# Two transformer blocks on one core: the taps of a 31-wide convolution become tiles of the weight stream

## The reference

```
u = rms_norm_2(h, norm_mix[i])
q, k, v, c, g = jnp.split(u @ w_in[i], splits, axis=-1)
... y_attn = window_attention(q, k, v, ...) @ w_attn_out[i]
c_val, c_gate = jnp.split(c, 2, axis=-1)
c = c_val * jax.nn.sigmoid(c_gate)                     # 256 tokens x 512 channels
c = depthwise_conv(c, conv_w[i], conv_b[i])            # 31 taps, each channel by itself
c = jax.nn.silu(layer_norm_2(c, conv_ln_g[i], conv_ln_b[i]))
y_conv = c @ w_conv_out[i]
g_attn, g_conv = jnp.split(jax.nn.sigmoid(g), 2, axis=-1)
h = h + (g_attn * y_attn + g_conv * y_conv) @ w_o[i]
```

## Time and profile before

| | us |
|---|---|
| median of three runs | 2175.07 (2174.5 to 2175.16) |
| profiled execution | 2176.42 |
| its span | 2174.4 |
| DVE busy | 1677.5 (77%) |
| ACT busy | 1263.8 (58%) |
| hi copies, 656, ACT | 689.0, 1.056 each |
| lo splits, 656, DVE | 792.9, 1.221 each |

### The profile page before, as it was taken

The page is one execution under the profiler, slowest core; times in us unless marked ns, Lnnn a source line. Parts: engine busy times, 40 slices in busy tenths (PEclk is TensorE's granted clock), DMA queues, the critical chain, the costliest instruction groups (busy, mean ns, idle before and its releaser), DMA issues.

```text
span 2174.4 us, 38816 instructions
## 1 busy us (share of the span) xinstructions
PE 2153.4 (99%) x16094; PEld 1967.3 (90%) x16094; DVE 1677.5 (77%) x2610; ACT 1263.8 (58%) x2098; POOL 13.1 (1%) x20
## 2 busy tenths in 40 slices
PE   8999999999999999999999999999999999999999
PEld 6898989999998998998888999988898889998888
DVE  7877599888876678877787677888678766978875
ACT  4754656555745556555555557665565545676554
POOL 0000000000000000000000000000000000000000
PEclk9999999999999999999999999999999999999999
DMA  9544566777644467655555533555555553355553
GB/s 363 200 163 170 171 232 244 246 242 274 225 146 165 138 232 223 211 176 188 181 188 192 179 123 117 203 187 192 186 181 188 191 185 135 119 165 206 189 189 131
DMA packets 116370, 415.12 MB, mean 191 GB/s; under 512 B 13105, under 2 KB 16561, under 8 KB 115682
## 3 DMA queue, kind: packets, MB, share of 16 engines
q1 hardware_dynamic: 116194, 412.63, 56.2%
HBM read 409.42 MB, written 3.16 MB: 190 GB/s over the span
## 4 chain that ended last, share of the span: by engine, by line
PE 93%; DVE 3%; ACT 2%; DMA 2%; issue 0%; SPq 0%; ACTq 0%
PE bank L198 92%; DMA raw<-W 2%; DVE lo L205 1%; ACT arena L250 1%; PE bank L202 1%; DVE arena L205 1%; ACT hi L250 0%; DVE arena L213 0%; DVE ada L222 0%; ACT L242 0%; DMA xT<-x 0%; ACT L250 0%; DVE h L205 0%; DVE ysl L205 0%; DVE sml L231 0%
## 5 line engine op out<-in xcount | busy, mean ns | idle before, releaser
L198 PE MATMUL bank<-h,hi 128*128 128x256 f32 (+1 forms) x5344 | 1223.1, 314 | 0.0
L250 ACT ACTIVATE hi<-raw 128x1024 fp32r<-128x1024 f32 x656 | 689.0, 1056 | 568.7 <-PE bank L198 500.6
L198 PE MATMUL bank<-h,lo 128*128 128x256 f32 x3440 | 986.2, 287 | 3.7 <-DVE h L205 3.6
L198 PEld LDWEIGHTS bank<-h,hi 128*128 128x128 f32 x5344 | 880.1, 190 | 67.1 <-issue 2.6
L205 DVE TENSOR_TENSOR lo<-raw,hi 128x1024 fp32r<-128x1024 f32 x656 | 792.9, 1221 | 92.6 <-ACT hi L250 91.8
L198 PEld LDWEIGHTS bank<-h,lo 128*128 128x128 f32 x3440 | 654.6, 190 | 15.8 <-issue 7.3
L198 PE MATMUL bank<-act,hi 128*128 128x512 f32 x1056 | 370.0, 393 | 0.0
L198 PE MATMUL bank<-act,lo 128*128 128x256 f32 x1056 | 294.7, 279 | 0.0
L198 PEld LDWEIGHTS bank<-act,hi 128*128 128x128 f32 x1056 | 197.9, 187 | 47.1
L198 PEld LDWEIGHTS bank<-act,lo 128*128 128x128 f32 x1056 | 197.9, 187 | 0.0
L198 PE MATMUL bank<-arena 64*64 64x64 f32 (+7 forms) x2674 | 196.9, 271 | 1.0 <-ACT arena L250 0.6
(11 more groups left out here) (150 smaller groups left out, 1915.9 us busy)
## 6 DMA issues: line engine op xcount, KB each, us to landing
raw<-W SPq DMA_DIRECT2D x664, 512.0 KB, 3.3
ada<-WA SPq DMA_DIRECT2D x80, 512.0 KB, 3.7
arena<-WA SPq DMA_DIRECT2D x16, 512.0 KB, 14.4
p_projected<-arena SPq DMA_DIRECT2D x2, 1024.0 KB, 7.8
arena<-scr SPq DMA_DIRECT2D x16, 128.0 KB, 4.9
arena<-p_projected SPq DMA_DIRECT2D x2, 1024.0 KB, 5.4
xT<-x SPq DMA_DIRECT2D x2, 512.0 KB, 5.1
arena<-lora SPq DMA_DIRECT2D x2, 512.0 KB, 9.8
```

The lines of the kernel that those rows point to most:

```text
L198: return self.done(lambda e: e.matmul(out, l, r, start=start, stop=stop, skip_group_check=True))
L250: return self.done(lambda e: e.activation(out, in_, f, scale=scale, **kw))
```

## The change

The 88 PE taps of the two layers become 88 tiles of the weight stream, two runs of 22 a layer. The host lays the 128 weights of a tap on the diagonal of a 128x128 tile; the tile comes by DMA and is split like any other. The values are split as well: ACT copies 266 columns of `Cb` to `Ch`, DVE writes the rest to `Cl`. ACT's diagonals and PE's float32 taps go. The order of the DVE taps stays; the sum for the first pair of groups comes at step 8, the one for the second pair after step 20. The runs stand in the main list, the first behind the factor column and the second between the last qkv group and v. A layer has 44 tiles, five and a half blocks, so between the first layer's runs and the second layer's the block borders lie four tiles off. On ACT the attention's chain is no longer put to the front.

```diff
+TW = S + CW - CV - 1
-NT2 = 2 * (44 * 8 + 22 * 8) + 30 * 8 + 32 + 32 + 64 + 64 + 16
+NT2 = 2 * (44 * 8 + 22 * 8) + 30 * 8 + 32 + 32 + 64 + 64 + 16 + 4 * 11
 def conv2_steps(l):
     for pair in (0, 2):
-        todo = [(m, j) for m in (pair, pair + 1) for j in range(CV, CW)]
-        built = []
         for j in range(0, CV, 2):
-            s += [("taps", pair, j)]
-            if j >= 4:
-                s += [("pe tap", pair, *t) for t in built.pop(0)]
-            built.append(todo[:3])
-            del todo[:3]
-            s += [("diag", pair, *t) for t in built[-1]] + ["next"]
-        s += [("conv sum", pair)]
+            s += [("taps", pair, j)] + [("conv sum", 0)] * ((pair, j) == (0, 14)) + ["next"]
+    s += [("conv sum", 2)]
...
-        s += [("mixer2", l), ("c", l, 0), ("c", l, 1), ("c", l, 2), ("conv2", l), ("c", l, 3), ("c last", l), ("rcol", l)]
-        s += [("qkv", l, p) for p in range(3)] + [("v2", l), ("qk norm", l), ("attention2", l)]
+        s += [("mixer2", l), ("c", l, 0), ("c", l, 1), ("c", l, 2), ("conv2", l), ("tap halves", l, (0, 1)), ("c", l, 3),
+              ("c last", l), ("rcol", l), ("taps", l, 0)]
+        s += [("qkv", l, p) for p in range(2)] + [("tap halves", l, (2, 3)), ("qkv", l, 2), ("taps", l, 2), ("v2", l), ("qk norm", l), ("attention2", l)]
...
+                elif what == "taps":                     # TensorE
+                    l, pr = q
+                    o = take(CONV, ("conv", l, pr))
+                    for m in (pr, pr + 1):
+                        pe.wait_ge(v_cv, ("tap halves", l, m))
+                        for j in range(CV, CW):
+                            wh, wl, ends = tile([("conv_w_2", l, j, ("diag", m))])
+                            om = t256(o, m - pr)
+                            ch, cl = (x[m % 3][:, j - CV:j - CV + 256] for x in (Ch, Cl))
+                            pe.mm(om, wl, ch, j == CV, False)
+                            pe.mm(om, wh, ch, False, False)
+                            i = pe.mm(om, wh, cl, False, j == CW - 1)
...
+                        v.tt(Cl[m % 3], Cb[:, m, CV:CV + TW], Ch[m % 3].bitcast(F32), SUB).then_inc(v_cv, ("tap halves", l, m))
...
-        a.act(diag[n % 8], C("ident"), ACT.Identity, scale=P("conv_w_2", l, j * 4 + m)).then_inc(
-            a_cv, ("diag", l, m, j))
...
+                        if m == 3:
+                            a.wait_ge(pe_main, ("conv", l, 0))
+                        a.act(Ch[m % 3], Cb[:, m, CV:CV + TW], ACT.Copy).then_inc(a_cv, ("tap high", l, m))
...
-                    f.chain(("att2", q[0]), att2_steps(q[0]), attention2(q[0]), True)
+                    f.chain(("att2", q[0]), att2_steps(q[0]), attention2(q[0]))
...
+        elif m[0] == "diag":
+            t = np.diag(w[k, m[1] * 128:(m[1] + 1) * 128])
```

More of the change, by code:

```diff
@@ L357, in conv2_steps @@
     for pair in (0, 2):
-        todo = [(m, j) for m in (pair, pair + 1) for j in range(CV, CW)]
-        built = []
         for j in range(0, CV, 2):
-            s += [("taps", pair, j)]
-            if j >= 4:
-                s += [("pe tap", pair, *t) for t in built.pop(0)]
-            built.append(todo[:3])
-            del todo[:3]
-            s += [("diag", pair, *t) for t in built[-1]] + ["next"]
-        assert not any(built), built
-        s += [("conv sum", pair)]
+            s += [("taps", pair, j)] + [("conv sum", 0)] * ((pair, j) == (0, 14)) + ["next"]
+    s += [("conv sum", 2)]
     return s + ["next", ("mean",), "next", ("square",), "next", ("var",), "next", ("norm",), ("silu",), "next", ("split",)]
@@ L604, in build @@
         cacc, cyc, cy2 = un(16, 4), un(20, 4), un(24, 4)
-        diag = [un(61, 4)[:, i * 128:(i + 1) * 128] for i in range(8)]
+        Ch, Cl = ([alias(name, at, 4)[:, i * TW:(i + 1) * TW] for i in range(3)] for name, at in (("Ch", 20), ("Cl", 24)))
         pf, pfh, pfl = un(49, 2), alias("pfh", 51, 2), alias("pfl", 57, 2)
@@ L1044, in conv2 @@
             def conv2(l):
-                taps = [0]
                 def step(what, *q):
[L1048 to L1058, removed]
+                    if what == "mean":
                         o = take(CONV, ("cmean", l))
@@ L1244, in tensor_program @@
                     f.chain(item, conv2_steps(q[0]), conv2(q[0]))
+                elif what == "taps":
[10 more added lines that the diff above has]
+                            i = pe.mm(om, wh, cl, False, j == CW - 1)
+                            names = ends + ([("conv", l, pr)] if (m, j) == (pr + 1, CW - 1) else [])
+                            if names:
+                                i.then_inc(pe_main, *names)
+                            if ends:
+                                f.tick()
                 elif what == "c":
@@ L1670, in step @@
                                     v.wait_ge(v_cv, ("tap", l, m, j - 1))
+                                    if (pr, j) == (0, 16):
+                                        v.wait_ge(v_cv, ("conv sum", l, 0))
                                     x = v.stt(o, Cb[:, m, j:j + 256], w(m, j), o, MUL, ADD)
@@ L1675, in step @@
                         o = cacc[:, pr * 256:(pr + 2) * 256]
-                        v.wait_ge(pe_cv, ("tap", l, pr + 1, CW - 1))
-                        v.wait_ge(v_cv, ("tap", l, pr + 1, CV - 1))
+                        v.wait_ge(pe_main, ("conv", l, pr))
+                        v.wait_ge(v_cv, ("tap", l, pr + 1, CV - 1 if pr else 15))
                         v.tt(o, o, ps(("conv", l, pr)), ADD).then_inc(v_cv, ("conv sum", l, pr), frees=("conv", l, pr))
@@ L1967, in vector_program @@
                     f.chain(item, conv2_steps(q[0]), conv2(q[0]))
+                elif what == "tap halves":
+                    l = q[0]
+                    for m in q[1]:
+                        v.wait_ge(a_cv, ("tap high", l, m))
+                        v.tt(Cl[m % 3], Cb[:, m, CV:CV + TW], Ch[m % 3].bitcast(F32), SUB).then_inc(v_cv, ("tap halves", l, m))
+                elif what == "taps":
+                    f.tiles(2 * (CW - CV))
                 elif what == "qkv":
@@ L2297, in conv2 @@
             def conv2(l):
-                built = [0]
                 def step(what, *q):
[L2301 to L2307, removed]
-                        a.act(diag[n % 8], C("ident"), ACT.Identity, scale=P("conv_w_2", l, j * 4 + m)).then_inc(
-                            a_cv, ("diag", l, m, j))
-                    elif what == "square":
+                    if what == "square":
                         a.wait_ge(v_cv, ("cmean", l))
@@ L2330, in conv2 @@
                 return step
-            conv_taps = [(m, j) for pr in (0, 2) for m in (pr, pr + 1) for j in range(CV, CW)]
             def merge(name, l, m, h):
@@ L2567, in scalar_program @@
                     f.chain(item, conv2_steps(q[0]), conv2(q[0]))
+                elif what == "tap halves":
+                    l = q[0]
+                    for m in q[1]:
+                        a.wait_ge(v_main, ("c", l, m))
+                        if m == 3:
+                            a.wait_ge(pe_main, ("conv", l, 0))
+                        a.act(Ch[m % 3], Cb[:, m, CV:CV + TW], ACT.Copy).then_inc(a_cv, ("tap high", l, m))
+                elif what == "taps":
+                    f.tiles(2 * (CW - CV))
                 elif what == "rcol":
```

## The result

The changed kernel takes 2198.07 us (median of four runs, 2196.62 to 2200.80) against 2175.11 for the kernel before (median of four); the ratio is 1.0106, with a 95% interval from 1.0093 to 1.0120. The forecast was 2193 us, inside 2182 to 2205. The profiled execution has a span of 2196.0 us, 21.6 more than before.

The account below looks back on a forecast made before the run. PE, busy 2153.4 of 2174.4 us, was taken as the bound. Gain -5.9, waits +1.5, +5.2, +3.7, +4.2, +5.5, +4.4, and -1.1 summed to +17.5 us: 2193 us, range 2182 to 2205.

Parts of the forecast that it names:

- PE's gain: PE work in both layers: 88 float32 taps go, 88 tap tiles come, taken as -5.9 us.
- The wait for the tap halves in layer 1: Ahead of layer 1's second tap run: PE waits 1.5 us for DVE's halves of c 2.
- First transposes: Attention's first half: with the taps' cover gone, PE waits for ACT's divide, 5.2 us in layer 0, 3.7 in layer 1.
- Second transposes: Attention's second half: ACT does the convolution's end inside it, so PE waits 4.2 us in layer 0, 5.5 in layer 1.
- the old wait: Second half, PE for DVE, 1.0 us before the change: stays in layer 0, counted 0.9, and goes in layer 1.
- Second output matmuls: Layer 0, behind the second transposes: PE waits 4.4 us for ACT's silu group, tanh and copies.
- rival (c): Clock falls to 1.2 GHz behind four of five long waits, 2.88 us a block, 11.5 in all: 2204 us; 13%.
- The granted clock of 1.00 throughout: Sign of the forecast: granted clock stays 1.00; under 1 in the waits' slices would be (c).
- (a): Rival: only the gain shows, ACT and DVE keep ahead of the faster PE: 2169 us; 7%.
- (b): Rival: DVE catches up during the v group, five long waits less 2 us each: 2183 us; 10%.
- (e): Rival: only the half-size gain and small waits that cancel, no change in time; 4%.
- (d): Rival: tap tiles no faster than the taps, +5.9 us on the forecast, 2199 us; 3%.

Follow-up runs that it names:

- the version that beats both: Changed kernel with attention ahead of the v group, one more border before both transposes, convolution's end six steps later, c 2 and 3 halves earlier: 2171.39 us, ratio 0.9984.

## Why the prediction was right, and where not

**PE's gain**: forecast 5.9 us; the version that beats both leaves 5 to 5.9. **The wait for the tap halves in layer 1**: 1.5 and 1.5. **First transposes**: 5.2 and 3.7 forecast, 4.9 and 3.8 measured. From the start of the qk norm (first row) to the divide's end it took 30.8 us, the number of the forecast; PE came after 26.1 in place of 25.6. The divide starts behind a wait for DVE's reciprocal, as the count of the chain had it:

```profile
1282.54 2.36 PE L199 MATMUL bank<-arena,cst 128*128 128x512 f32 x6
...
1310.06 3.30 ACT L251 ACTIVATE arena<-arena,sml 128x256 f32<-128x256 f32 x8 [1.25 <-DVE sml L220]
...
1337.76 1.28 ACT L251 ACT_TABLE_LOAD   x1
1339.06 0.47 ACT L251 ACTIVATE arena<-bank,cst 128x256 f32<-128x256 f32 x1
1339.55 1.28 ACT L251 ACT_TABLE_LOAD   x1
1340.84 0.42 ACT L251 ACTIVATE arena<-arena 128x256 f32<-128x256 f32 x1
1341.16 1.04 ACT L251 ACTIVATE hi<-raw 128x1024 fp32r<-128x1024 f32 x1
1342.11 3.28 ACT L251 ACTIVATE arena<-arena,sml 128x256 f32<-128x256 f32 x8
```

**Second transposes**: 4.2 and 5.5 forecast, 5.2 and 5.6 measured. The rows from 1337.76 on are the convolution's variance between the exponentials and the divide, as the order had it. The divide ended 24.8 us after the second scores (forecast 24.2). PE came after 19.8 (forecast 20.0): the old wait, kept at 0.9 in layer 0, had gone, but PE's own work took 0.7 more than counted. With the 0.15 us from the divide's end to the transposes these make the 1.0. The drain that the Trainium skill (ScalarE: Activation LUTs, "What ACT_TABLE_LOAD costs") adds to each switch shows nowhere here: the instruction behind each of these two starts 0.01 to 0.02 us after the load's end. **Second output matmuls**: 4.4 forecast, 2.5 measured. With the clock held up they waited 4.3, so the chain was right, and PE was late by the 1.8 us that the clock cost just ahead of them.

**The step that failed** is the separation of the forecast from rival (c). "The granted clock of 1.00 throughout" was wrong: it fell behind all four waits for the transposes. The rival was right that it falls and too high in its price, 2.88 us a fall: that is a whole block at the lower level, and PE worked there for 3.4 to 4.9 us, of which half is lost, 1.7 to 2.4 us. So the clock, which the sum had at nothing, cost 7.9 us. With both, forecast waits and clock, the sum would have been 17.5 + 7.9 - 1.8 = +23.6 us; the medians differ by 23.0. The time alone does not tell the two apart: it lies 5.1 us above the forecast and 5.9 below the rival's 2204. That it fell inside the range in spite of the clock, which no term of the forecast had in it, was in part luck; only the rows show which part of each was right. The earlier trace rows are waits of PE's weight loads; PE's own in that stretch are 1.4 and 1.5 us. They did not tell how the clock takes a wait of 4 us in steady work, because there was none to see, and a chance of 13% for it was too low. The Trainium skill (TensorE: Matmul & The Clock Gate, "Part 1: The HAM clock gate") said that an idle engine is put to half rate; here the trace agrees, with granted clocks of 0.51 to 0.63 behind waits of 3.8 to 5.6 us.

**The other rivals.** (a), (b) and (e) fell with the waits at their full size; (d) with tap tiles at 0.364 us. The range held the time because the waits were nearly right; with the clock in the sum its middle would have been right as well.

## What to carry to other kernels

Work taken from an engine that is 99% busy is not all won: it was also the time in which the other engines' chains ran. Take the engine's time from one hand-over to the next, subtract the work removed, and set it against the length of the other engines' chain between the two; what the chain is longer by comes back as a wait. Whoever shortens the bounding engine's work should also move the hand-overs by as many steps, and then look at the next hand-over, since a single one that is moved can pass its wait on. And long waits of TensorE cost more than they last: here 19.4 us of waits at the transposes cost another 7.9 us in clock.

## What the runs showed of the hardware

- Behind waits of 3.8 us and more in the second block the granted clock fell to 1.2 GHz every time: 18 waits of 3.8 to 8.2 us in six profiles, four in each of two profiles of the changed kernel. Behind 1.5 us it did not. In between it went both ways: behind the same wait of 2.03 us at the first transposes it fell in one kernel (transposes 3.50 us) and not in another (1.95 us), behind 2.5 us it did not fall, and behind 2.7 us it did in three kernels.
- Behind each such wait PE worked 3.1 to 5.9 us at the lower level, so the same program with nearly the same waits lost 7.9 us in one execution and 10.3 in another.
- A plain float32 matmul with a 128x128 weight and one column costs 0.22 us of PE between the tiles of the stream, half of the 0.43 us with 256 columns.
